# The residual kept with features on partitions, and the norms between the parts made without transposes, in a 14-part fp32 program on one core

## What is computed

```python
def rms_norm(x, g):
    xf = x.astype(jnp.float32)
    y = xf * lax.rsqrt(jnp.mean(xf * xf, axis=-1, keepdims=True) + EPS)
    return (y * g.astype(jnp.float32)).astype(x.dtype)
...
        h = rms_norm(x, g_mix[i])
...
        gates = jax.nn.sigmoid(h @ w_branch_gate[i]).reshape(b, s, N_BRANCHES, D_MODEL)
        merged = jnp.sum(gates * jnp.einsum('bsnc,ncd->bsnd', branches, w_branch[i]), axis=2)
        x = x + merged @ w_out[i]
...
        x = x + expert_choice_moe(rms_norm(x, g_moe[i]), w_router[i], w_exp_gate[i], w_exp_up[i], w_exp_down[i])
...
        ple_gate = jax.nn.sigmoid(rms_norm(x, g_ple[i]) @ w_ple_gate[i])
        x = x + ple_gate * (p[i] @ w_ple[i])
...
    return rms_norm(x, g_final)
```

```python
            x = x + fox_mixer(rmsnorm(x, att_norm_g[j]), att_w_in[j], att_b_f[j], att_w_out[j])
...
            x = x + hgrn2_mixer(rmsnorm(x, hgrn_norm_g[j]), hgrn_w_in[j],
...
        x = x + conv_ffn(rmsnorm(x, ffn_norm_g[layer]), ffn_w_up[layer], ffn_conv_w[layer],
                         ffn_conv_b[layer], ffn_w_down[layer])
```

## Time and profile before

| | us |
|---|---|
| median of three executions (3668.59 to 3678.15) | 3676.7 |
| the profiled execution | 3678.49 |
| its span in the trace | 3676.6 |
| PE busy | 3460.1, 94% of the span |
| DVE busy | 1609.6, 44% |
| ACT busy | 1129.2, 31% |
| POOL busy | 17.6, under 1% |
| PE clock granted, mean | 0.975 of full speed |

### The profile page before, as it was taken

The page is one execution under the profiler, slowest core; times in us unless marked ns, Lnnn a source line. Parts: engine busy times, 40 slices in busy tenths (PEclk is TensorE's granted clock), DMA queues, the critical chain, the costliest instruction groups (busy, mean ns, idle before and its releaser), DMA issues. The chain is left out here.

```text
span 3676.6 us, 43580 instructions
## 1 busy us (share of the span) xinstructions
PE 3460.1 (94%) x18220; PEld 2454.5 (67%) x18220; DVE 1609.6 (44%) x2489; ACT 1129.2 (31%) x1771; POOL 17.6 (0%) x24
## 2 busy tenths in 40 slices
PE   8989997999978989997999998899999999989999
PEld 5767885444438767877444437676788878868887
DVE  3654542111134564553111114434666655366656
ACT  4553322000013454231101002444432344443333
POOL 0000000000000000000000000000000000000000
PEclk9999998999998999997999999899999999999999
DMA  4112245999972212235899991412223222113222
GB/s 167 52 51 72 72 173 206 420 420 419 420 278 84 69 39 72 72 90 204 364 420 419 420 389 64 132 58 69 69 93 102 92 81 81 58 58 107 94 92 80
DMA packets 324737, 617.83 MB, mean 168 GB/s; under 512 B 10736, under 2 KB 212208, under 8 KB 324544
## 3 DMA queue, kind: packets, MB, share of 16 engines
q1 hardware_dynamic: 324544, 615.05, 45.0%
HBM read 610.79 MB, written 4.23 MB: 167 GB/s over the span
## 5 line engine op out<-in xcount | busy, mean ns | idle before, releaser
L481 PE MATMUL bank<-h_hi,w_hi 128*128 128x512 f32 x1816 | 731.6, 403 | 21.9 <-PEq L157 12.8
L483 PE MATMUL bank<-h_hi,w_lo 128*128 128x512 f32 x1816 | 719.8, 396 | 0.0
L482 PE MATMUL bank<-h_lo,w_hi 128*128 128x512 f32 x1816 | 719.7, 396 | 0.0
L286 DVE TENSOR_TENSOR w_lo<-w_raw,w_hi 128x2048 fp32r<-128x2048 f32 (+3 forms) x207 | 423.8, 2047 | 251.8 <-ACT w_hi L278 251.2
L2020 PE MATMUL bank<-expert_w,gathered 128*64 128x512 f32 x2048 | 448.4, 594 | 0.0
L278 ACT ACTIVATE w_hi<-w_raw 128x2048 fp32r<-128x2048 f32 (+3 forms) x207 | 355.0, 1715 | 278.9 <-PE bank L483 248.1
L481 PEld LDWEIGHTS bank<-h_hi,w_hi 128*128 128x128 f32 x1816 | 343.3, 189 | 118.7 <-issue 28.0
L483 PEld LDWEIGHTS bank<-h_hi,w_lo 128*128 128x128 f32 x1816 | 343.0, 189 | 82.9
L482 PEld LDWEIGHTS bank<-h_lo,w_hi 128*128 128x128 f32 x1816 | 343.5, 189 | 80.5 <-issue 1.9
L2020 PEld LDWEIGHTS bank<-expert_w,gathered 128*64 128x64 f32 x2048 | 144.3, 137 | 296.6 <-issue 296.4
L2020 PE MATMUL bank<-expert_w,hidden_t 128*64 128x512 f32 x1024 | 230.2, 602 | 7.9 <-DMA expert_w<-in_w_exp_down 7.9
(11 more groups left out here) (429 smaller groups left out, 4536.7 us busy)
## 6 DMA issues: line engine op xcount, KB each, us to landing
expert_w<-in_w_exp_gate SPq DMA_DIRECT2D x64, 2048.0 KB, 21.7
expert_w<-in_w_exp_up SPq DMA_DIRECT2D x64, 2048.0 KB, 19.4
expert_w<-in_w_exp_down SPq DMA_DIRECT2D x64, 2048.0 KB, 22.8
w_raw<-in_ffn_w_up SPq DMA_DIRECT2D x44, 1024.0 KB, 5.1
w_raw<-in_w_branch_gate SPq DMA_DIRECT2D x64, 512.0 KB, 3.7
w_raw<-in_w_in SPq DMA_DIRECT2D x22, 1024.0 KB, 5.1
w_raw<-in_ffn_w_down SPq DMA_DIRECT2D x22, 1024.0 KB, 4.9
w_raw<-in_hgrn_w_in SPq DMA_DIRECT2D x16, 1024.0 KB, 5.4
```

The source lines that it names most:

```text
L286: dve.tensor_tensor(self.w_lo[n % 2][:, 0:e], self.raw[n % self.RAW][:, 0:e], self.w_hi[n % 2][:, 0:e].bitcast(F32), ALU.subtract).then_in ...
L481: pe.matmul(out, st[0], mv[0], start=(j == 0), stop=False)
L482: pe.matmul(out, st[0], mv[1], start=False, stop=False)
L483: last = pe.matmul(out, st[1], mv[0], start=False, stop=(j == len(g.steps) - 1))
```

## The change

`x` is held as 8 blocks of 128 features by 512 tokens, from the first load to the last store; the host gives it in this layout and turns the output back. With it:

- The first tile of each part still needs the norm. **Norm** replaces `norm_stage`, `NextNorm` and the router's part: ACT squares each feature block as it is done, GpSimd adds squares 1 to 5 into square 0, PE sums over partitions with 12 small fp32 matmuls of one column, ACT roots, DVE takes the reciprocal, PE spreads it with 4 matmuls, DVE scales 8 blocks, ACT and DVE split them.

```diff
+    def square(self, act, kt):
+        act.wait_ge(*self.added(kt))
+        act.activation(self.sq[:, kt, :], self.v.x[:, kt, :], ACT.Square).then_inc(*self.squares.inc())
+    def gather_squares(self, eng):
+        for kt in range(1, 6):
+            eng.wait_ge(*self.squared(kt + 1))
+            if kt >= 2:
+                eng.wait_ge(*self.gathered_to(kt - 1))
+            eng.tensor_tensor(self.sq[:, 0, :], self.sq[:, 0, :], self.sq[:, kt, :], ALU.add).then_inc(*self.gathered.inc())
+    def sums(self, pe):
+        pe.wait_ge(*self.gathered_to(5))
+        for n, kt in enumerate((0, 6, 7)):
+            if n:
+                pe.wait_ge(*self.squared(kt + 1))
+            for tb in range(TB):
+                last = pe.matmul(self.bank[:, tb:tb + 1], self.sq[:, kt, tb * P:(tb + 1) * P], self.v.ones[:, 0:1], start=(n == 0 and tb == 0), stop=(n == 2 and tb == TB - 1))
+        last.then_inc(*self.summed.inc())
...
+    def spread_to(self, pe, bank, per_token):
+        for tb in range(TB):
+            last = pe.matmul(bank[:, tb * P:(tb + 1) * P], per_token[:, tb:tb + 1].to_broadcast([P, P]), self.v.ident[:], start=True, stop=True)
+        last.then_inc(*self.rows.inc())
...
+    def scale(self, dve):
...
+        for kt in range(KT):
+            dve.scalar_tensor_tensor(out=v.h_plain[:, kt, :], in0=v.x[:, kt, :], scalar=self.gains[:, kt:kt + 1], in1=self.bank[:],
+                                     op0=ALU.mult, op1=ALU.mult).then_inc(*self.scaled.inc())
```

```diff
+                    late = n == count - 1 and len(t.groups) > 4
+                    if (n + 1 < count or following) and not late:
                         ring.rest(dve, n0 + n + 1)
                     if t.pre_dve:
...
+                        if lead and n < lead.tile:
+                            lead.dve_during(dve, i)
+                        if late and following and i == 1:
+                            ring.rest(dve, n0 + n + 1)
...
+    def pe_before_tile(self, pe):
+        self.sums(pe)
+        self.spread(pe)
```

```diff
     for c in range(D // 256):
-        groups = [Group([((a_hi[:, kt, tb * P:(tb + 1) * P], a_lo[:, kt, tb * P:(tb + 1) * P]), (kt * 256, 256)) for kt in range(kts)],
...
+def k_part_tile(v, w, g, halves, needs):
+    groups = [Group([((b * D + kt * P, P), halves[b]) for b in range(2)], S, None, add_to_x(v, kt)) for kt in range(KT)]
     return Tile([(0, w_rows(w, 0, D, k0=g * 256, kt=2))], groups, needs=needs)
```

```diff
-    NT, RING, EARLY = 12, 8, 4
+    NT, RING, EARLY = 12, 9, 4
```

```diff
+                    ps, part = v.ps[6 + h][:].rearrange("p (k s) -> p k s", s=P), slice(4 * h, 4 * h + 4)
+                    dve.tensor_scalar(ye_hi[:, part, :], ps, weight[i % 2][:], None, ALU.mult).then_inc(y_high.sem, 1)
+                    dve.wait_ge(*at(y_high, i, h + 1))
+                    dve.scalar_tensor_tensor(out=ye_lo[:, part, :], in0=ps, scalar=weight[i % 2][:], in1=ye_hi[:, part, :].bitcast(F32),
+                                             op0=ALU.mult, op1=ALU.subtract).then_inc(y_ready.sem, 1)
...
+                    for tb in range(TB):
+                        last = pe.matmul(v.ps[4][:, tb * NE:(tb + 1) * NE], v.x[:, kt, tb * P:(tb + 1) * P], wr_g[:, kt, :],
+                                         start=(kt == 0 and tb == 0), stop=(kt == KT - 1 and tb == TB - 1))
                 last.then_inc(*logits.inc())
+                norm.sums(pe)
+                for n in range(5):
+                    turn(n)
                 pe.wait_ge(*normed.ge(1))
                 for tb in range(TB):
...
+                    last = pe.transpose(v.ps[5][0:NE, tb * P:(tb + 1) * P], aff[:, tb, :], v.ident[:])
                 last.then_inc(*turned.inc())
+                for n in (5, 6, 7):
+                    pe.wait_ge(*xs_ready.ge(n - 4))
...
+                    pe.matmul(scatter_bank(i, k)[:], ye_hi[:, k, :], onehot_t[i % 2][:], start=True, stop=False)
+                    pe.matmul(scatter_bank(i, k)[:], ye_lo[:, k, :], onehot_t[i % 2][:], start=False, stop=True).then_inc(sc_sum.sem, 1)
```

```diff
+    def split_rest(self, dve):
+        self.v.ring.rest(dve, self.v.ring.tiles)
+        dve.wait_ge(*self.p_high.ge(1))
+        dve.tensor_tensor(self.p_lo[:], self.p_t[:], self.p_hi[:].bitcast(F32), ALU.subtract)
...
+    def pe_during(self, pe, i):
+        if i == 3:
+            pe.wait_ge(*self.added(KT - 1))
+        if i == 4:
+            self.sums(pe)
+        if i == 5:
+            self.spread(pe)
...
+    def act_start(self, act):
+        for kt in range(KT):
+            self.square(act, kt)
+        self.root_table(act)
...
+    def act_during(self, act, i):
+        if i == 4:
+            self.root(act)
...
+    def dve_start(self, dve):
+        self.add(dve)
+    def dve_during(self, dve, i):
+        if i == 4:
+            self.reciprocal(dve)
```

```diff
+    def tail_pe(self, pe, k):
+        kt = self.kt_of.get(k)
+        if kt:
+            self.part(pe, kt - 1)
...
+    def pe_before_tile(self, pe):
+        self.part(pe, KT - 1).then_inc(*self.summed.inc())
+        pe.wait_ge(*self.rstd.ge(1))
+        self.spread_to(pe, self.bank, self.v.rstd2)
+        self.spread_to(pe, self.v.ps[6], self.v.rstd)
```

```diff
+            for kt in range(KT):
+                sp.wait_ge(*ready.ge(kt + 1))
+                sp.dma_start(v.out[kt * P:(kt + 1) * P, :], v.x[:, kt, :]).then_inc(*stored.dma())
+            sp.wait_ge(*stored.ge(16 * KT))
...
+                                         op0=ALU.mult, op1=ALU.mult).then_inc(*ready.inc())
+        @block.tensor
+        def _(pe):
```

887 lines of the change are left out of this document (430 added, 457 removed).

## The result

The changed kernel takes 3652.7 us (median of four, 3652.0 to 3657.5) against 3675.7 (median of four runs): a ratio of 0.9943, with an interval of 0.9926 to 0.9961. It is faster by 0.6%, and the forecast was 1.8%: 3611.5 us, range 3589 to 3641. The direction was right, the size was not. The profiled span fell from 3676.6 to 3650.3, so 26.3 us are to be accounted for, where the sum had 65.2.

What follows compares the result with a forecast made beforehand. PE was taken to bound the kernel, with DMA also full in the MoE. The stage terms summed to -65.2 us, taking the span from 3676.6 to 3611.4 and the median to 3611.5 us, range 3589 to 3641.

Steps and rivals of the forecast that it cites:

- A: PLE in both layers, from the last expert product to the last PLE product: -14.1 us each, -28 together.
- E: The MoE's experts in both layers: transfers set the end, a ninth slot saves a tile, -5.1 us each, -10.2 together.
- Rival 2: The MoE gives nothing: transfers don't stay full or the last tiles come as late as now; 3622 us, chance 0.13.
- F: The router in both layers, from the mixer's last product to the first expert product: +1.9 us each, +4 together.
- G: Three seams at NextNorm, from the start of the last tile to the first row: 18.3 us each, -13.3 together.
- B: The seam from PLE to the mixer of layer 1: 8.6 us instead of 19.2, -10.6.
- rival 1: Gains at the seams come back through the clock: three cold seams, 3 us each, +9, 3620 us; chance 0.12.
- rival 3: GpSimd and DVE hinder each other: a w_lo holds up one add in nine chains, 18 us, 3630; chance 0.09.
- Rival 4: GpSimd's chains are the bound: the whole gain gone at 2.85 us an add, 3683 us at 3.0; chance 0.03.
- H: The start, up to the first dense product: 41.5 us instead of 39.0, +2.5.
- I: The end, from the last product to the span's end: 14 us instead of 7.0, +7.
- D: The mixers' last product, 192 products of 512 columns replacing 384 of 256: -1.8 us for both layers.

Runs made afterwards that it cites:

- e8: The changed kernel with pads that put all nine expert slots and the weight ring on multiples of 256 bytes: 3632.9 us.
- e11: The changed kernel with each norm summing only the gathered square over partitions, 8 passes instead of 24, once all squares are there: 3635.3 us.
- e5: The changed kernel with the router's first 20 transposes set among the logits instead of behind the sums: 3663.8 us.
- e7: The changed kernel without six of the seven sums over partitions that the double norm makes inside PLE's last four tiles: 3648.9 us.
- e6: The changed kernel with the next part's w_lo made ahead of the last tile again, not after its second group: 3658.2 us.
- e13: The changed kernel with ACT's load of the root's table at the first square of a last tile, not behind the seventh, except in PLE: 3654.1 us.
- e14: The changed kernel with the root's table loaded early and the next part's w_lo after the last tile's first group instead of the second: 3653.9 us.
- e12: The changed kernel with the relative bias tables loaded first and ACT's first w_hi behind six of the eight copies: 3637.9 us.
- e10: The kernel before with only a pad of 128 bytes ahead of x, leaving two of eight expert slots on multiples of 256 bytes: 3690.1 us.

## Why the prediction was wrong, point by point

It was right on what bounds the kernel, and on PLE in layer 0 and the seam to fox: A gave 14.6 there for 14.1, GpSimd's chain was covered (it ended at E+15.9, the sums began at E+17.5), and C gave 14.3 for 14.4. That A was met so closely is luck in part: the first gate row came at E+28.5 for 30.2, the products behind it took 45.4 us for 44.2, and in six of the other runs the same stage gave 11.6 to 12.5. The misses, by size:

**E, the experts, 20.7 us of the 38.9 missed.** The step that failed is "a tile of 2.1 MB at 420 GB/s is 5.0 us": I took the rate of the rows as the chip's, and it was a rate of these addresses. The mechanism of the step (transfers set the end, a slot more saves a tile) is confirmed: with the addresses on 256 bytes again (e8) each stage falls by 5.1 and 5.0 against the kernel before, and 5.1 was forecast. The bounds of E ran from -7 to nothing; no row excluded a slower rate, and a resource at a share of 1.02 can also get slower. Rival 2, by which the experts give nothing, came nearer but named neither cause: the transfers stayed full, and the last expert tile landed not as late as before but 6.2 us later behind the first product (459.3 for 453.1).

**F, the routers, 9.2 us.** I had seen the lower clock coming and added 1.9 each; 7.1 and 5.9 came. The step that failed is "at a clock that has fallen by then": it puts the low clock at the sums and transposes and leaves the logits, more than half of which ran at the full clock before. Now the clock falls 2.4 and 3.4 us behind the mixer's last product instead of 8.8, and nearly all 88 passes take 0.2 us, 18 us in all. The prediction gives L+17.8 for the affinities without its parts, and 23.3 and 22.7 came. With the fall at its latest, 5 us behind, other runs had 21.1, still 3 too many. e11 puts the 16 passes of sums at 3.4 us, and e5 shows that mixing in the transposes doesn't help.

**A in layer 1, 9.1 us.** I took both layers for equal. The seven sums of the double norm are products within PLE's tiles, 56 passes at 0.12, and none of them stands in my sum. I had not asked who makes these sums when GpSimd doesn't (e7: 4.8 for 48 passes). With the wait of 2.6 for the first square this is most of the 9.1.

**G and B, 9.0 us.** The windows of the earlier trace rows are now 21.1, 20.4 and 20.3, forecast 18.3. The sentence that failed is "only the 8 of the last square lie behind it": the sums stand in the next block, so all 24 passes lie behind it (e11: 1.6 to 2.0 of the seam, 2.7 behind PLE). Then rival 1, whose condition came true at all three seams: in the kernel before, the clock was at its full level from the last product to the first row (the 0.93 of the earlier trace rows comes from the last tile ahead of it), now it falls 3.5 to 4.9 us behind the last product and is still down at the first row, and the spread takes 2.1 instead of 1.0. What the clock alone costs there no run separates. And rival 3's premise came true at the three seams, without its price: a GpSimd add took 1.30 and not 1.09, which with its wait is the 1.4 of a group. There was no slack of 0.3. The delay of the first add, 2.61 beside DVE's `w_lo`, went through to the end of the chain, 1.46 us behind the last product; ACT's table load and dummy root end at 1.50 there, and to take either away, or both, gained nothing (e6, e13, e14). Rival 4 is out: 1.30 is far from 2.85. The row of 1.09 had operands that repeat one row of 128; these don't.

**H and I, 4.8 us.** Of H's 2.7, 2.0 are the landing of the tables, at 18.0 for the 16 foretold, and the rest is the seam behind them. I's 2.1 are the same seam, longer by sums and spread: the first scale comes 7.9 us behind the last product, for 6. The start would have been a gain of 7 with its loads in another order (e12); I had treated that order as given.

**Gains not forecast, 13.5 us.** Without them the miss would have been larger, so they are luck. D gave 5.8 for 1.8, of which the clock is a part: in the kernel before, that stage began with 6 us at 0.50 granted in both layers, after the change in layer 1 alone. The mixers' other tiles took 7.1 less and ffn 1 2.4. Products of the gates start every 0.229 us instead of 0.232; in the second block the first products of an MLP are faster (0.227 for 0.233) and its last ones slower (0.233 for 0.227). The cause stays open. e10, which moves all buffers alike by 128 bytes, leaves these numbers as they are; but in e8, where the pads also move some buffers against others, the gates start every 0.227 and the mixers' branch products every 0.229 instead of 0.233. So where the buffers stand is not ruled out.

## What to carry over

When a term rests on a rate, ask what in the change could alter the rate itself, and look at where buffers start whenever the layout of memory moves: here two pads, of 128 and 32 bytes, were worth 20 us. Count what a merged step still computes, engine by engine, and mark in which block each piece of it stands; what stands behind a barrier is on the path. Narrow matmuls at a seam are doubly dear, by their number and because they ran at the lower clock here. And when a forecast is met, look at other runs of the same stage before believing its parts.

## What was not expected of the hardware

- Transfers from HBM to SBUF of 4 KB rows at full load: 421 GB/s with all destinations on multiples of 256 bytes, 420 with six of eight, 414 with two of eight, 409 with none, at the same share of the DMA engines, 1.02 to 1.03.
- fp32 matmuls of one and of 16 columns with a 128x128 stationary operand: 0.12 us a pass at the full clock and 0.2 to 0.22 at the lower one, whatever the columns. The granted clock fell to 0.5 in the routers 2.2 to 5.2 us behind the last dense product and at the three seams 3.5 to 4.9 behind it, while PE was busy with them without a gap, but behind a pause of 1.4 and 1.8 us. Which of the two, pause or narrow passes, brings it down was not separated.
- GpSimd, an fp32 add of two 128x512 operands: 1.30 us alone, 2.61 at the three seams, where a DVE subtraction of two SBUF operands (2.28) had begun 0.8 us earlier. The Trainium skill (SBUF — State Buffer, "Who interferes with whom") says that a DVE instruction with two SBUF inputs contends with a GpSimd one that reads SBUF; these rows agree, and no run gained by undoing it.
- In the changed kernel the windows give a granted clock of 1.00 up to 47 us, while matmuls of 512 columns start every 0.43 us; the trace has no row of the clock before 47.3, and from there on they start every 0.23. There the start times, and not the clock's column, tell the pace.
